# Splitting the weight pieces of the mixers in halves, between the attention steps

## The reference: what is computed

```
def first_block(x, p, ...):
    for i in range(2):
        h = x + 0.5 * swiglu(rms_norm(x, norm_ffn1[i]), w_ffn1_in[i], w_ffn1_out[i])
        u = rms_norm(h, norm_mix[i])
        q, k, v, c, g = jnp.split(u @ w_in[i], splits, axis=-1)
        y_attn = window_attention(q, k, v, sink[i], rel_bias) @ w_attn_out[i]
        c = silu(layer_norm(depthwise_conv(c_val * sigmoid(c_gate), conv_w[i], conv_b[i]), ...))
        y_conv = c @ w_conv_out[i]
        h = h + (g_attn * y_attn + g_conv * y_conv) @ w_o[i]
        h = h + 0.5 * swiglu(rms_norm(h, norm_ffn2[i]), w_ffn2_in[i], w_ffn2_out[i])
        x = h + (p[i] @ w_pe_proj[i]) * sigmoid(rms_norm(h, norm_pe[i]) @ w_pe_gate[i])

def second_block(x, ...):
    for layer in range(2):
        proj = rmsnorm(x, ln1_g[layer]) @ w_in[layer]
        out_a = mixer_dilated(...); out_b = mixer_mla(...); out_c = mixer_diff(...)
        x = x + jnp.concatenate([out_a, out_b, out_c], axis=-1) @ w_o[layer]
        x = x + jnp.square(relu(rmsnorm(x, ln2_g[layer]) @ w_up[layer])) @ w_down[layer]
    return rmsnorm(x, final_g)
```

## Time and profile before

| | us |
|---|---|
| median of three runs | 1935.22 |
| lowest and highest | 1934.88, 1939.82 |
| the profiled execution, time | 1939.92 |
| its span | 1938.1 |
| busy: PE, DVE, ACT, POOL | 1850.0, 1117.6, 885.3, 24.8 |
| mean granted TensorE clock | 0.974 |

### The profile page before, as it was taken

The page is one execution under the profiler, slowest core; times in us unless marked ns, Lnnn a source line. Parts: engine busy times, 40 slices in busy tenths (PEclk is TensorE's granted clock), DMA queues, the critical chain, the costliest instruction groups (busy, mean ns, idle before and its releaser), DMA issues.

```text
span 1938.1 us, 27635 instructions
## 1 busy us (share of the span) xinstructions
PE 1850.0 (95%) x11400; PEld 1649.3 (85%) x11400; DVE 1117.6 (58%) x1568; ACT 885.3 (46%) x1205; POOL 24.8 (1%) x31
## 2 busy tenths in 40 slices
PE   5999999999999999999899999998899999889998
PEld 4899887789988999887779998787798988779896
DVE  4554577665545655467666554666455556646553
ACT  4344455544434444345554443565453545544342
POOL 0000000000000000000000000000000000000000
PEclk8999999999999999999899999998899999899999
DMA  6555442255545454543245555433245543224541
GB/s 243 196 196 177 177 147 109 107 182 174 186 163 211 157 183 177 184 174 109 102 158 180 177 182 185 159 119 109 86 169 183 181 157 135 92 86 173 194 174 44
DMA packets 45740, 305.19 MB, mean 157 GB/s; under 512 B 5008, under 2 KB 6032, under 8 KB 11824
## 3 DMA queue, kind: packets, MB, share of 16 engines
q1 hardware_dynamic: 45616, 303.43, 44.1%
HBM read 300.26 MB, written 3.15 MB: 157 GB/s over the span
## 4 chain that ended last, share of the span: by engine, by line
PE 73%; issue 13%; DVE 7%; ACT 5%; DMA 1%; DVEq 0%; SPq 0%; POOLq 0%; POOL 0%; ACTq 0%
PE ps L439 11%; PE ps L440 11%; PE ps L441 11%; PE ps L467 11%; PE ps L468 11%; PE ps L469 11%; ACT whi L929 3%; DVE wlo L1399 3%; DVE acc L1547 2%; PE ps L750 1%; PE ps L774 1%; PE ps L487 1%; PE ps L563 1%; PE ps L759 1%; ACT tmp L1201 1%
## 5 line engine op out<-in xcount | busy, mean ns | idle before, releaser
L1399 DVE TENSOR_TENSOR wlo<-raw,whi 128x2048 fp32r<-128x2048 f32 (+4 forms) x292 | 646.6, 2216 | 499.2 <-ACT whi L929 498.9
L929 ACT ACTIVATE whi<-raw 128x2048 fp32r<-128x2048 f32 (+4 forms) x292 | 540.3, 1851 | 358.6 <-PE ps L441 251.5
L467 PE MATMUL ps<-x_hi,wlo 128*128 128x256 f32 x2048 | 588.6, 287 | 19.2 <-DVE wlo L1399 19.2
L468 PE MATMUL ps<-x_lo,whi 128*128 128x256 f32 x2048 | 585.4, 286 | 0.0
L469 PE MATMUL ps<-x_hi,whi 128*128 128x256 f32 x2048 | 585.2, 286 | 0.0
L467 PEld LDWEIGHTS ps<-x_hi,wlo 128*128 128x128 f32 x2048 | 399.4, 195 | 26.9 <-DVE wlo L1399 20.7
L468 PEld LDWEIGHTS ps<-x_lo,whi 128*128 128x128 f32 x2048 | 399.7, 195 | 0.2
L469 PEld LDWEIGHTS ps<-x_hi,whi 128*128 128x128 f32 x2048 | 399.1, 195 | 0.0
L440 PE MATMUL ps<-wlo,hid_hi 128*128 128x512 f32 x608 | 241.7, 398 | 0.0
L439 PE MATMUL ps<-whi,hid_hi 128*128 128x512 f32 x608 | 239.7, 394 | 0.0
L441 PE MATMUL ps<-whi,hid_lo 128*128 128x512 f32 x608 | 239.5, 394 | 0.0
(11 more groups left out here) (244 smaller groups left out, 1530.1 us busy)
## 6 DMA issues: line engine op xcount, KB each, us to landing
raw<-in_w SPq DMA_DIRECT2D x264, 1024.0 KB, 4.8
raw<-in_w SPq DMA_DIRECT2D x12, 768.0 KB, 4.2
raw<-in_w SPq DMA_DIRECT2D x8, 512.0 KB, 3.2
raw<-in_w SPq DMA_DIRECT2D x4, 576.0 KB, 3.6
line_scratch<-line SPq DMA_DIRECT2D x8, 256.0 KB, 2.9
raw<-in_w SPq DMA_DIRECT2D x2, 864.0 KB, 4.4
bias<-line_scratch SPq DMA_DIRECT2D x1, 1536.0 KB, 9.3
h<-in_x SPq DMA_DIRECT2D x1, 1024.0 KB, 5.3
```

The costliest lines, as they stand in the source:

```text
L467: e.matmul(o, wl, x_hi[:, c, :], start=first and n == 0 and m % 2 == 0, stop=False)
L468: e.matmul(o, wh, x_lo[:, c, :], start=False, stop=False)
L929: e.activation(w_at(whi, j, 0, n), raw[:, j % RAW, 0:n], ACT.Copy).then_inc(s_hi, 1)
L1399: e.tensor_tensor(w_at(wlo, j, 0, m), raw[:, j % RAW, 0:m], f32(w_at(whi, j, 0, m)), ALU.subtract).then_inc(s_lo, 1)
```

## The change

`halved(j)` holds for each piece with an even number of chunks whose splitting lies beside a mixer piece: 78 of the 292, 64 of them 2048 columns wide, twelve 1536 and two 1152. ACT and DVE split such a piece in two instructions. The first half comes where the whole stood, the second behind the first tick in `use`. Semaphores count two per piece; PE waits before each chunk for the half that it lies in, and SP for both halves. In the mixer of the second block the `low` of `va` moves: one tick, then the first half, the second rotary turn, one tick, then the second half. In DVE's `bg` of the first block the attention goes ahead of the taps. The ring of diagonals grows from 4 to 16 and lies in the second half of `thg`.

```diff
+MIXERS = ("w_in", "w_attn_out", "w_conv_out", "w_o", "w_in_2", "mla_w_uq_2", "mla_w_ukv_2", "w_o_2")
+def halved(j):
+    return j > AHEAD and ORDER[j - AHEAD][0] in MIXERS and len(ORDER[j][2]) % 2 == 0
+PARTS = []
+for _j, _p in enumerate(ORDER):
+    _n = size(_p)
+    PARTS += [(_j, 0, _n // 2, 1), (_j, _n // 2, _n // 2, 1)] if halved(_j) else [(_j, 0, _n, 2)]
+def split_value(j, off):
+    return 2 * j + (1 if halved(j) and off < size(ORDER[j]) // 2 else 2)
...
+        diag = flat(thg[:, 1, :, :]).rearrange("p (i n) -> p i n", i=16)
...
             def rows(spec, jobs, need, mid=None, done=True, steps=1):
-                e.wait_ge(s_lo, j + 1)
                 for n, (off, N, op, xc, bk, first, last) in enumerate(jobs):
+                    e.wait_ge(s_lo, split_value(j, off))
...
-                        e.wait_ge(s_cv, n - 4)
+                        e.wait_ge(s_cv, n - 16)
...
-            def low(upto):
-                while split[0] < min(upto + 1, len(ORDER)):
-                    j = split[0]
-                    m = size(ORDER[j])
-                    e.wait_ge(s_hi, j + 1)
-                    e.tensor_tensor(w_at(wlo, j, 0, m), raw[:, j % RAW, 0:m], f32(w_at(whi, j, 0, m)), ALU.subtract).then_inc(s_lo, 1)
+            def low(upto, half=False):
+                upto = min(upto, len(ORDER) - 1)
+                while split[0] < len(PARTS) and (PARTS[split[0]][0] < upto or PARTS[split[0]][0] == upto and not (half and PARTS[split[0]][1])):
+                    j, off, n, count = PARTS[split[0]]
+                    e.wait_ge(s_hi, split_value(j, off))
+                    e.tensor_tensor(w_at(wlo, j, off, n), raw[:, j % RAW, off:off + n], f32(w_at(whi, j, off, n)), ALU.subtract).then_inc(s_lo, count)
                     split[0] += 1
             def use(spec, ticks=None, mid=None, steps=1):
-                low(NUM[spec] + AHEAD)
+                low(NUM[spec] + AHEAD, True)
                 n = len(spec[2]) if ticks is None else ticks
                 for i in range(n):
                     if i % 2 == 1 and i < n - 1:
                         tick(steps)
                         if mid is not None:
                             mid()
+                        low(NUM[spec] + AHEAD)
+                low(NUM[spec] + AHEAD)
                 tick(steps)
...
-                bg.append(att)
+                bg.insert(0, att)
...
                 rope(l, "k", ka[:, 0, :], 6, 64, 0, 32, 0, out2(l, "k", 0))
+                tick()
+                low(NUM[va_[0]] + AHEAD, True)
+                rope(l, "k", ka[:, 1, :], 6, 64, 0, 32, 1, out2(l, "k", 1))
+                tick()
                 low(NUM[va_[0]] + AHEAD)
-                tick()
-                rope(l, "k", ka[:, 1, :], 6, 64, 0, 32, 1, out2(l, "k", 1))
-                tick(3)
+                tick(2)
```

More of the change, by code:

```diff
@@ L256, in build @@
             ("qT", [128, 4, 256], F32), ("kT", [128, 256], F32),
-            ("cpad", [128, 4 * 286], F32), ("acc", [128, 4, 256], F32), ("diag", [128, 4, 128], F32)])
+            ("cpad", [128, 4 * 286], F32), ("acc", [128, 4, 256], F32)])
         fill.close()
@@ L342, in build @@
         yt = M1["cpad"][:, 0:1024].rearrange("p (t n) -> p t n", t=2)
-        thg, qs, qn, kv, qT, kT, acc, diag = (M1[n] for n in ("thg", "qs", "qn", "kv", "qT", "kT", "acc", "diag"))
+        thg, qs, qn, kv, qT, kT, acc = (M1[n] for n in ("thg", "qs", "qn", "kv", "qT", "kT", "acc"))
+        diag = flat(thg[:, 1, :, :]).rearrange("p (i n) -> p i n", i=16)
         qa, ka, va, rt, cq, kr, vc, kb, vb, qbT, kbT, mix = (
@@ L457, in columns_ @@
                 first, last = spec[2][0] == 0, spec[2][-1] == 7
-                e.wait_ge(s_lo, j + 1)
                 for n, c in enumerate(spec[2]):
+                    e.wait_ge(s_lo, split_value(j, n * 512))
                     e.wait_ge(s_xlo, xv(name, l, c))
@@ L562, in conv_taps @@
                     e.wait_ge(s_dgc, n)
-                    e.matmul(O[:, 0:256], diag[:, tap % 4, :], pad[:, 3, tap:tap + 256], start=tap == 0, stop=tap == TAPS - 1).then_inc(s_cv, 1)
+                    e.matmul(O[:, 0:256], diag[:, tap % 16, :], pad[:, 3, tap:tap + 256], start=tap == 0, stop=tap == TAPS - 1).then_inc(s_cv, 1)
                     if tap % 5 == 4:
@@ L919, in drain, with high @@
                     bg.remove(g)
-            def high(upto):
-                while split[0] < min(upto + 1, len(ORDER)):
-                    j = split[0]
+            def high(upto, half=False):
+                upto = min(upto, len(ORDER) - 1)
+                while split[0] < len(PARTS) and (PARTS[split[0]][0] < upto or PARTS[split[0]][0] == upto and not (half and PARTS[split[0]][1])):
+                    j, off, n, count = PARTS[split[0]]
                     e.wait_ge(s_raw[j % RAW], 16 * (j // RAW + 1))
@@ L927, in high @@
                         e.wait_ge(s_used, j - SPLIT + 1)
-                    n = size(ORDER[j])
-                    e.activation(w_at(whi, j, 0, n), raw[:, j % RAW, 0:n], ACT.Copy).then_inc(s_hi, 1)
+                    e.activation(w_at(whi, j, off, n), raw[:, j % RAW, off:off + n], ACT.Copy).then_inc(s_hi, count)
                     split[0] += 1
             def use(spec, ticks=None, mid=None, end=True, steps=1):
-                high(NUM[spec] + AHEAD)
+                high(NUM[spec] + AHEAD, True)
                 n = len(spec[2]) if ticks is None else ticks
@@ L940, in use @@
                             mid()
+                        high(NUM[spec] + AHEAD)
+                high(NUM[spec] + AHEAD)
                 if end:
@@ L1022, in conv_taps @@
                     n = TAPS * l + tap + 1
-                    if tap >= 4:
-                        e.wait_ge(s_cv, n - 4)
-                    e.activation(diag[:, tap % 4, :], ident, ACT.Copy, scale=k("conv_w", (l * 4 + 3) * 31 + tap)).then_inc(s_dgc, 1)
+                    if tap >= 16:
+                        e.wait_ge(s_cv, n - 16)
+                    e.activation(diag[:, tap % 16, :], ident, ACT.Copy, scale=k("conv_w", (l * 4 + 3) * 31 + tap)).then_inc(s_dgc, 1)
                     if tap % 5 == 4:
@@ L2063, in load @@
                     if j >= RAW:
-                        e.wait_ge(s_hi, j - RAW + 1)
-                        e.wait_ge(s_lo, j - RAW + 1)
+                        e.wait_ge(s_hi, 2 * (j - RAW) + 2)
+                        e.wait_ge(s_lo, 2 * (j - RAW) + 2)
                     src = w_d[OFFS[j]:OFFS[j + 1]].rearrange("(p n) -> p n", p=128)
```

## The result

The changed kernel takes **1889.3 us** (median of 4 runs, 1886.4 to 1890.8), the kernel before 1937.5 on the same chip: a ratio of 0.975, 95% interval 0.9728 to 0.9771. That is 48 us, where the sum said 37. The profiled execution took 1886.4 us, 53.5 less than that of before; the sum was made from the rows of the profiled executions, so 53.5 is what it has to be held against.

The account below looks back on a forecast made before the run. PE was taken as the bound, busy 1850.0 of 1938.1 us. Terms 9.0 + 2.6 + 10.0 + 6.6 + 9.2 = 37.4 took the profiled 1939.9 to 1902.5; forecast 1901, own range 1888 to 1914, overall 1882 to 1924.

Parts of the forecast that it names:

- First mixers, attention (9.0): First block's mixers: PE's waits on the ACT copy (6.9) and attention output (2.1) all go, 9.0 us; bounds 0 and 9.0.
- The round of 4.5 us: First mixers: scores 1.07, exponentials 1.19, ACT half 1.06, DVE half 1.22, together 4.5 us, below PE's step of 5.29.
- Diagonals (2.6): First block's mixers: PE's waits for diagonals fall from 5.5 to about 2.9 us, winning 2.6; bounds -0.4 and 5.5.
- Clock, first mixers (10.0): First block's mixers: of 11.9 us lost to PE's lowered clock, 10.0 come back as waits go; bounds 0 and 11.9.
- Second block, waits (6.6): Second block's mixers: copy waits fall from 10.9 to 8.2 us a layer, mixer ends save 0.6; together 6.6 us.
- Clock, second block (9.2): Second block's mixers: of 24.2 us lost to PE's lowered clock, 15 stay and 9.2 come back; bounds 0 and 24.2.
- Fixed costs of the halves (0): 78 cut pieces: 16 us more work on ACT and 12 on DVE, costed at nothing because idle time covers them.
- The slower rival: Rival, chance 0.06: in first mixers the taps fall into the round, 6.5 us against 5.29, costing 39 us; 1962 us.
- The fixed costs eat the second block: Rival, chance 0.13: fixed costs and the round remove the second block's 15.8 us and a quarter of first mixers'; 1922 us.
- The second block clears as well: Rival, chance 0.15: DVE is idle 40% in the second block, so its waits and clock win about 22 more; 1879 us.

## Why the prediction was right, and where its steps were not

The range held the time and the sign was right, but the forecast came in near the fast edge of its own range (1888 to 1914). The sum was 11 us short of the medians and 16 short of the profiled executions, and four of its five terms were too small. Two of its mechanisms were wrong in part, so that the range held is in part luck: half of the sum, the 9.0 and the 10.0 of the first mixers, was worked out from a round of halves and comes with whole pieces as well. One slip doesn't matter: halfway between 1902.5 and 1897.8 is 1900.2, not 1901.

*First mixers, attention (9.0).* Right in size: all of it went. Half right in cause. The round of 4.5 us is in the trace (315.06 less 310.59 is 4.47). But the run with the taps' place alone shows that it isn't needed: the waits vanish with whole pieces and rounds of 7.54 and 2.90. I had compared a single round with a single step, where by these rounds it is the pair that has to fit.

*Diagonals (2.6).* 4.8 us of waits went, 0.7 is left where I left 2.9. At the place of the earlier trace rows 0.34 is left (0.4 to 1.0 said), and the other wait, for which I left 0.8 or more, is gone. The four-diagonal run puts most of it on the halves: 5.5 to 2.1 without the ring, and the ring brings the 1.4 more, which the time doesn't show. It needs the halves apart: with the ring and the halves together 2.6 are left, with the ring and whole pieces 4.2.

*Clock, first mixers (10.0).* All 11.9 came back; the clock is 1.00 in both.

*Second block, waits (6.6).* The direction was right, the size wrong: 11.2 came. I let the copy's waits fall from 10.9 to 8.2 a layer, new ones among them; they fell to 6.1 (5.15 on the copy, 0.95 on ACT's `cq`). The place of the earlier trace rows went to 1.96 (2.4 said), the rest to 4.1 (5.8 said). The new waits are two a layer, not three, and the second halves were priced as standing in the way between two steps, 3.3 us with ACT and DVE in series. At the place of the earlier trace rows they do stand there, and that price was right. DVE takes the scores at 1292.42, waits for ACT's second half, and takes the next scores only at 1296.41, 3.99 us later and 3.1 us after ACT has begun the exponentials (1293.30):

```profile
1295.27 1.23 DVE L1423 TENSOR_TENSOR wlo<-raw,whi 128x1024 fp32r<-128x1024 f32 x1 [2.00 <-ACT whi L951]
```

With the halves together it is 1.58 us from scores to scores here, with whole pieces 0.79, and PE's wait is 0.71 and 0.91 in place of 1.96. What was priced too high are the other places. That DVE's half runs beside ACT's second was a term only at the mixer's end (0.6; 0.8 measured). The run with the halves together shows that this term, 0.85 us at the longest waits and 0.2 to 0.8 at the others, is what the cut brings.

*Clock, second block (9.2).* The term that was mis-sized most: I left 15 us and 5.9 are lost (3% of 147 and 1% of 148). So 18 came back by these rounded shares, 15.6 by PE's busy time in the four stretches of the earlier trace rows and above (144.63 + 145.04 to 137.06 + 137.04). The granted clock is still 0.62 for 4 us behind the wait of 1.96, and 0.53 for 7 us behind the wait of 1.77:

```profile
1302.00:1306.00 4.00, 3.90 (x16) 3.44 (x15) 2.51 (x11) 2.07 (x8) 0.00 (x0) 0.62 0.01 2
1319.00:1326.00 7.00, 7.00 (x26) 6.02 (x26) 2.13 (x7) 3.77 (x12) 0.00 (x0) 0.53 0.00 0
1650.00:1654.00 4.00, 4.00 (x19) 3.93 (x18) 1.60 (x6) 2.78 (x7) 0.00 (x0) 0.60 0.00 0
```

The same wait in the second mixer (1.76) is followed by a short stretch at 0.60, and behind the waits of 0.6 us the clock is 1.00. With the waits of 3.75 and 2.1 of the whole pieces the two mixers stood at 0.92 and 0.93, which is 23 us lost. How the clock follows from the waits is not settled: the halves-together kernel has a wait of 2.90 in both mixers, which stood at 0.94 and 0.99, and the first of them, with the same instructions, at 0.97 in the profile of the change and at 0.94 in that of the halves alone.

*Fixed costs of the halves (0).* Right, with more room than needed: not even 206 further cuts show. The price was also too high. Two halves back to back take 1.99 and 2.36 us, 0.08 and 0.07 more than the whole, where twice the duration of one gives 0.21 and 0.16, since the next instruction's record begins some 0.1 us before the end of the one ahead. Of the rule I quoted from the Trainium skill ("VectorE: DVE Perf Modes", the section on the TRN2 errata: a fixed cost for each SBUF-source instruction, of some 150 cycles, which at its 0.96 GHz makes an estimate of 156 ns) this means that back to back no more than half of it shows here, and on a path that PE waits for the cut gained. The Trainium skill's other rule, in "Perfetto Trace Analysis", section "Optimizing Scalar/DVE Operations" (where the two engines aren't full but make others idle, broken-up instructions may let work complete sooner), is the one that this case bears out: DVE at 60%, ACT at 47%, and PE's longest wait 0.85 us shorter.

*The slower rival.* Its mechanism is real, in a kernel that isn't this one: with halves and the taps in front the round is 6.43 us (6.5 computed) and PE waits 18.3 us in the first block. The price of 39 us was too high: it counted 16 late steps a layer, and only the eight heads have such a round. What excluded it is the one line that puts the taps last. *The fixed costs eat the second block* fell with the halves everywhere. *The second block clears as well* (1879) was nearer to the truth than I gave it: of its 22 us some 11 to 13 came, 4.6 of waits and 6 to 9 of clock.

How the 48 us divide, by runs: the taps' place alone 18; with sixteen diagonals and the moved copy 33 (ratio 0.9834); the cut brings the rest, 16 to 19, nearly all in the second block. The moved copy is worth some 3 us beside the halves (a difference within the intervals), and 7 to 9 with whole pieces (8.4 and 9.5 in the second block, less 1.0), where it saves the whole low part; no run has it alone. The placing of each half behind a half step, which gave the change its name, brought nothing that these runs can tell.

## What to carry to other kernels

When two engines work one after the other on each tile and a third waits behind them, cut the tile for that pair: the second engine starts half a tile earlier, here for 0.85 us of PE's longest waits and some 0.1 us of extra work on each engine. Compare rounds of side work with PE's steps over a few of them together, not one by one, and first take out of the round what depends on nothing in it (the taps: 18 us for one line). Where an engine stands idle ahead of an instruction that waits, look at what is queued behind it: the two ACT moves at stage ends gave 8 us on top of the whole change, beyond the intervals (1880.9 against 1889.3), while reordering an engine that is full in that stretch only moved the waits.

## What the runs showed that was not expected

The granted clock of one and the same stretch of code differs between kernels that differ elsewhere only (0.94 and 0.97 in the second block's first mixer; over the whole second block 6.4 us), so single profiles can't tell such a share of the gain. The splits by stage above have to be read with that much slack; what the text calls a gain of a run rests on the medians and their intervals. Durations of rows overstate what an instruction costs in a series by some 0.1 us each on ACT and DVE (1.99 for two of 1.05; 2.36 for two of 1.22). And more cuts made the wait at the end of the embedding shorter as well, 2.63 to 1.78, 0.85 us once more.
